# Expert stage of a one-core diffusion layer: twenty weight buffers, one 80-row scatter per expert, a last down product in the shape of the others

## The reference, cut to what matters

```python
def expert_choice_ffn(h, w_router, w_gate, w_up, w_down):
    cap = 2 * n // N_EXPERTS                       # 64 of 512 latent, 16 of 128 context rows per expert
    aff = softmax(h @ w_router)
    gates, idx = top_k(swapaxes(aff, 1, 2), cap)   # each expert picks its own rows
    xe = h[idx]
    ye = (silu(xe @ w_gate) * (xe @ w_up)) @ w_down * gates
    return zeros(n, d).at[idx].add(ye)
x = x + gate2 * expert_choice_ffn(h, ...)
y = rms_norm(x, g_final)
```

## Time and profile before

| | |
|---|---|
| device time, median of 3 runs | 1182.05 us |
| the profiled execution's own time | 1175.39 us |
| its span, first to last instruction | 1173.6 us |
| TensorE busy | 1104.6 us (94%) |
| VectorE busy | 449.3 us (38%) |
| ScalarE busy | 367.7 us (31%) |
| GpSimd busy | 200.1 us (17%) |
| DMA in the expert stage | 395 to 411 GB/s in nearly every slice of 29 us |
| the chain that ended last | PE 71%, DMA 16%, DVE 5% |

### The profile page before, as it was taken

The page is one execution under the profiler, slowest core; times in us unless marked ns, Lnnn a source line. Parts: engine busy times, 40 slices in busy tenths (PEclk is TensorE's granted clock), DMA queues, the critical chain, the costliest instruction groups (busy, mean ns, idle before and its releaser), DMA issues.

```text
span 1173.6 us, 28123 instructions
## 1 busy us (share of the span) xinstructions
PE 1104.6 (94%) x12399; PEld 797.6 (68%) x12399; DVE 449.3 (38%) x755; ACT 367.7 (31%) x818; POOL 200.1 (17%) x237
## 2 busy tenths in 40 slices
PE   6999999999999999999979999999999998999883
PEld 4679877778876777777857777777777555555540
DVE  4574458889957142244373110111111110101113
ACT  4333337777743212112244012222221121012103
POOL 1343450000000000010014022222222221121210
PEclk9999999999999999999997999999999999999997
DMA  9952242111052434549398999999999999999985
GB/s 365 305 199 72 73 94 47 31 35 34 9 221 69 153 137 144 179 155 358 126 367 312 411 395 397 395 395 396 396 396 395 396 399 411 398 385 397 379 319 196
DMA packets 117016, 303.46 MB, mean 259 GB/s; under 512 B 27817, under 2 KB 34818, under 8 KB 116386
## 3 DMA queue, kind: packets, MB, share of 16 engines
q1 hardware_dynamic: 104256, 273.21, 61.3%
q0 software_dynamic: 11472, 20.99, 6.9%
q10 hardware_dynamic: 1170, 7.48, 1.5%
HBM read 276.78 MB, written 19.64 MB: 253 GB/s over the span
## 4 chain that ended last, share of the span: by engine, by line
PE 71%; DMA 16%; DVE 5%; ACT 3%; issue 2%; SPq 2%; ACTq 0%; POOL 0%; DVEq 0%; POOLq 0%
PE ps L1196 29%; DMA late<-in_w_exp_down_dram 10%; PE ps L765 9%; PE ps L766 9%; PE ps L767 9%; PE ps L991 3%; PE ps L975 2%; DVE neg_max L1810 2%; SPq L710 2%; DMA raw<-in_w_exp_down_dram 2%; PE ps L1014 1%; DMA x_dram<-xn_p 1%; PE ps L1010 1%; DVE q_lo_t L1802 1%; DMA raw<-in_w_in_dram 1%
## 5 line engine op out<-in xcount | busy, mean ns | idle before, releaser
L1196 PE MATMUL ps<-late,xe 128*32 128x256 f32 x3648 | 200.3, 379 | 1.0 <-DMA late<-in_w_exp_gate_dram 1.0
L1196 PEld LDWEIGHTS ps<-late,xe 128*32 128x32 f32 x3648 | 133.6, 110 | 64.7 <-DMA late<-in_w_exp_gate_dram 2.9
L1563 ACT ACTIVATE xe<-xt,mod_t,scale 128x64 f32<-128x64 f32 x240 | 78.0, 413 | 184.8 <-DVE gates L2107 184.8
L2127 DVE SCALAR_TENSOR_TENSOR y_q<-ps,gates,gate_q 128x256 f32<-128x256 f32 x45 | 19.0, 478 | 303.2 <-PE ps L1196 303.2
L2349 POOL DMA_INDIRECT x_dram<-y_q,rows x45 | 71.4, 1587 | 373.6 <-DVE y_q L2127 364.4
L765 PE MATMUL ps<-w_hi,ht 128*128 128x512 f32 (+1 forms) x320 | 124.8, 390 | 0.0
L766 PE MATMUL ps<-raw_lo,ht 128*128 128x512 f32 (+1 forms) x320 | 121.8, 381 | 0.0
L767 PE MATMUL ps<-w_hi,ht 128*128 128x512 f32 (+1 forms) x320 | 121.8, 381 | 0.0
L1196 PE MATMUL ps<-late,ht 128*32 128x256 f32 x1920 | 109.4, 380 | 9.0 <-DMA late<-in_w_exp_down_dram 8.9
L1196 PEld LDWEIGHTS ps<-late,ht 128*32 128x32 f32 x1920 | 68.3, 110 | 47.4 <-DMA late<-in_w_exp_down_dram 14.8
L1196 PE MATMUL ps<-raw,xe 128*32 128x256 f32 x1632 | 92.2, 381 | 3.4 <-DMA raw<-in_w_exp_gate_dram 3.4
(11 more groups left out here) (308 smaller groups left out, 1687.1 us busy)
## 6 DMA issues: line engine op xcount, KB each, us to landing
late<-in_w_exp_down_dram SPq DMA_DIRECT2D x44, 1024.0 KB, 21.0
late<-in_w_exp_up_dram SPq DMA_DIRECT2D x40, 1024.0 KB, 18.4
late<-in_w_exp_gate_dram SPq DMA_DIRECT2D x36, 1024.0 KB, 18.8
raw<-in_w_exp_gate_dram SPq DMA_DIRECT2D x18, 1024.0 KB, 18.8
raw<-in_w_in_dram SPq DMA_DIRECT2D x16, 1024.0 KB, 5.7
raw<-in_w_exp_up_dram SPq DMA_DIRECT2D x16, 1024.0 KB, 18.4
raw<-in_w_exp_down_dram SPq DMA_DIRECT2D x14, 1024.0 KB, 21.2
raw<-in_w_mod_dram SPq DMA_DIRECT2D x12, 1024.0 KB, 6.9
```

Of the source, the lines that this page charges most:

```text
L1196: mm = pe.matmul(out[32 * q:32 * q + 32, :], x[:, k, :], columns_of(w, q), start=(k == 0), stop=(k == KD - 1))
L1563: a = act.activation(xe[:, e % 2, sets, k, :], xt[:, sets, k, :], ACT.Identity, scale=scale2[:, k, v:v + 1], bias=mod_t[:, 24 + k, v:v + 1])
```

## The change

- **Ring.** `ESLOT` is 20. The four new slots lie where token and routing buffers were, so their first chunks (16 to 19) wait until the rows of all experts are known (`s_rows`, 5) and the normed tokens are stored, no longer for chunks 0 to 3 to be used up.
- **Scatter.** The residual is scattered in whole rows: one indirect DMA per expert of 80 rows of 4 KB in place of three of 128 quarter rows. For it VectorE writes the result as [80 x 1024] (`y_row`): quarter q of set v goes from partitions 32q.. to partitions 32v.., in twelve multiplies of 32 (or 16) partitions x 256 columns in place of three of 128 x 256.
- **Hidden.** `hidden` becomes `activations`: multiply and turn by sets, in the order 0, 2, 1.
- **Down blocks.** They go set by set through all four chunks (before: two sets together, then the third). d15 is such a block too, in banks 0 to 2, and `s_front` counts its sets.
- **Order at the end.** d14 stands ahead of g15 and u15, where it stood between them. VectorE norms two tiles ahead of expert 15's `activations` and three behind it; the last rows are finished by quarters.
- **Loops.** None left on SP, ScalarE and VectorE. Several semaphores are merged or renamed, the DRAM copy of the gates goes, and g_final is loaded behind scatter 14.

```diff
-ESLOT = 16
+ESLOT = 20
+EXPERT_BLOCKS = [("g", 0), ("u", 0)]
+for _n in range(1, NE - 1):
+    EXPERT_BLOCKS += [("g", _n), ("d", _n - 1), ("u", _n)]
+EXPERT_BLOCKS += [("d", NE - 2), ("g", NE - 1), ("u", NE - 1), ("d", NE - 1)]
+FIRST_CHUNK = {b: 4 * n for n, b in enumerate(EXPERT_BLOCKS)}
...
-                                                                 32768, 40960, 49152))]
+                                                                 32768, 40960, 49152, 97280, 105472, 113664, 141312))]
...
+                    elif c == 16:
+                        sp.wait_ge(s_x2out, 16 * (NT + 1))
+                        sp.wait_ge(s_rows, 5)
+                    elif c == 19:
+                        sp.wait_ge(s_post, MODS_DONE + 1)
+                        sp.wait_ge(s_ss2, 2 * NT)
...
+                if kind == "d":
+                    last = n == NE - 1
+                    for at_set, v in enumerate((0, 2, 1)):
+                        pe.wait_ge(s_ht2, SETS * n + at_set + 1)
+                        out = bank(v, 0, 256) if last else bank(7, 0, 256) if v == 2 else bank(6, 256 * v, 256 * v + 256)
                         for k in range(KD):
                             c = c0 + k // 2
+                            if at_set == 0:
+                                pe.wait_ge(s_slot[c % ESLOT], expert_raw(c))
+                            mm = set_product(out, ht2[:, v], expert_chunk(c)[:, k % 2, :], quarter_columns, k)
...
+            def activations(n):
+
+                dve.wait_ge(s_half, done("u", n))
+                dve.wait_ge(s_silu2, n + 1)
+                for at_set, v in enumerate((0, 2, 1)):
+                    dve.tensor_tensor(h_t[:, v, :], h_t[:, v, :], bank(3 + v, 0, 256), ALU.mult).then_inc(s_dve, 1)
+                    dve.wait_ge(s_dve, own())
+                    t = dve.transpose(ht2[:, v, :, :].rearrange("p k b -> p (k b)"), h_t[:, v, :]).then_inc(s_ht2, 1)
+                dve.sem_inc(s_hm, 1)
+
+            def output_piece(n, v, q):
+                count = 32 if v < 2 else CAPC
+                src = slice(32 * q, 32 * q + count)
+                b, o = (v, 0) if n == NE - 1 else (6 + v // 2, 256 * (v % 2))
+                return dve.scalar_tensor_tensor(y_row[n % 2][32 * v:32 * v + count, 256 * q:256 * q + 256],
+                                                bank(b, o, o + 256, src), gates[src, n % EG, v:v + 1],
+                                                gate2_q[src, v // 2, :], ALU.mult, ALU.mult)
+
+            def output(n):
+
+                dve.wait_ge(s_half, done("d", n))
+                dve.wait_ge(s_xgt, n + 1)
...
                 for v in range(SETS):
-                    dve.scalar_tensor_tensor(y_q[:, e % 2, v, :], bank(6 + v // 2, 256 * (v % 2), 256 * (v % 2) + 256),
-                                             gates[:, e % EG, v:v + 1], gate2_q[:, v // 2, :], ALU.mult, ALU.mult)\
-                       .then_inc(s_yg, 1)
+                    for q in range(4):
+                        y = output_piece(n, v, q)
+                y.then_inc(s_yg, 1)
+
+            for n in range(NE - 1):
+                if n:
+                    output(n - 1)
+                tokens_turned(n + 1)
+                activations(n)
+
+            output(NE - 2)
...
-                for v in range(SETS):
-                    pool.indirect_dma_start(x1_quarters[:, :], bass.IndirectOffsetOnAxis(ap=rows[:, v, n:n + 1], axis=0),
-                                            y_q[:, n % 2, v, :], None, compute_op=ALU.add).then_inc(s_scat, 16)
+                pool.indirect_dma_start(x1_dram[:, :], bass.IndirectOffsetOnAxis(ap=rows_t[0:EROWS, n:n + 1], axis=0),
+                                        y_row[n % 2][0:EROWS, :], None, compute_op=ALU.add).then_inc(s_scat, 16)
```

More of the change, by code:

```diff
@@ L597, in expert_rows, with done @@
             return w[0, n, 2 * q * P:(2 * q + 2) * P, :].rearrange("(k p) n -> p k n", p=P)
[L599 to L618, removed]
+        def done(kind, n):
+            return DENSE_HALVES + FIRST_CHUNK[kind, n] + 4
         @block.sync
@@ L678, in _ @@
                         sp.dma_start(x_n[:, t, :], xs[t] if t < NTL else x_prompt[0]).then_inc(s_x[t], 16)
-            def weights(i, kind, e, c0, first):
+            for kind, n in EXPERT_BLOCKS:
                 for q in range(4):
-                    c = c0 + q
-                    if first and c == 2:
+                    c = FIRST_CHUNK[kind, n] + q
+                    if c == 2:
                         for t in range(NT):
@@ L1257, in side_product @@
-            def side_product(c, f, k):
-                pe.wait_ge(s_slot[c % ESLOT], expert_raw(c, NG))
-                w, flags = expert_chunk(c)[:, k % 2, f * NW:(f + 1) * NW], {"start": k == 0, "stop": k == KD - 1}
-                for v in range(SETS):
-                    mm = pe.matmul(bank(6 + f, rows=slice(32 * v, 32 * v + 32)), ht2[:, v, k, :], w, **flags)
-                if f and k % 2 == 1:
-                    mm.then_inc(s_half, 1)
-                elif f == 0 and k == KD - 1:
-                    mm.then_inc(s_front, 1)
@@ L1584, in _ @@
                                    bias=mod_t[:, 24 + k, v // 2:v // 2 + 1]).then_inc(s_xe0, 1)
-            groups(act, body)
+            for n in range(NE):
+                silu(n)
+                if n + 1 < NE:
+                    scaled(n + 1)
             def finish_rms(t):
@@ L2109, in hidden @@
[L2109 to L2122 removed]
+                dve.tensor_copy(gates[:, n % EG, :].unsqueeze(2), xg[:, b, :, 256 + n:257 + n]).then_inc(s_xgt, 1)
@@ L2131, in body @@
-            def body(i, first, last):
-                for e in range(EG):
-                    if e or not first:
-                        output(i, e - 1)
-                    if not last or e < EG - 1:
-                        tokens_turned(i, e + 1)
-                    else:
-                        dve.wait_ge(s_xgt, NE)
-                        for v in range(SETS):
-                            own_rows = slice(32 * v, 32 * v + (32 if v < 2 else CAPC))
-                            dve.tensor_copy(gate_z[own_rows, :], gates[own_rows, EG - 1, v:v + 1]).then_inc(s_rows, 1)
-                    hidden(i, e)
+                    for q in range(4):
+                        y = output_piece(n, v, q)
@@ new lines, in _ @@
+            finish(0)
+            finish(1)
+            activations(NE - 1)
+            for t in range(2, NT):
+                finish(t)
+            dve.wait_ge(s_scat, 16 * (NE - 2))
+            for at_set, v in enumerate((0, 2)):
+                dve.wait_ge(s_front, at_set + 1)
+                for q in range(4):
+                    output_piece(NE - 1, v, q).then_inc(s_dve, 1)
+            own(8)
+            dve.wait_ge(s_front, 3)
+            dve.wait_ge(s_xl2, 16)
+            for q in range(4):
+                output_piece(NE - 1, 1, q).then_inc(s_dve, 1)
+                dve.wait_ge(s_dve, own())
+                last_sums(q)
```

290 lines of the change are left out of this document (106 added, 184 removed).

## The result

| | before | changed |
|---|---|---|
| median of 4 runs each | 1180.07 us | 1202.03 us (1199.01 to 1204.45) |
| ratio | | 1.0182, 95% interval 1.0163 to 1.0200 |
| profiled execution / its span | 1175.39 / 1173.6 us | 1204.45 / 1202.6 us |

The change makes the kernel 1.8% slower. The profile of before and that of the changed kernel come from different chips, as experiment 1 shows, so a few microseconds between them need not come from the change. Both kernels run again on one chip (experiment 1) gave 1.0185 (1.0156 to 1.0213).

The account below looks back on a forecast made before the run. TensorE's own pace bound the kernel, with DMA close; lengthening the chain to `xe` would stall it. u15's end at 1169.5 plus a 31.8 tail made 1201.3 against 1173.6; +27.7 on median 1182.05 gave 1209.8 us, range 1174 to 1219.

Parts of the forecast that it names:

- chain longer by: Chain beside TensorE, from down block through output pieces to `xe`: 5.0 us longer a round, with 2.1 us to spare.
- TensorE stands: Start of the gate blocks g2 to g14: TensorE idles 2.9 us, 13 times, waiting for ScalarE's `xe`.
- a round without a fall of the clock: Expert rounds of three blocks: 34.0 us each instead of 31.08.
- falls: TensorE's clock drops to half behind the stalls in two rounds of three: 8.7 x 1.65 = 14.3 us, bounds 0 and 21.5.
- end of u15: End of expert 15's up block: at 1169.5 us, against 1138.1 before.
- The pieces are held: VectorE's output pieces each start only after the last ended: 0.508 us each, twelve 6.10 us; chance 0.75.
- the gain of slots and scatter: Four more weight slots issue chunks 8.8 us earlier and scatter relieves DMA, but no stall is left to fill.
- The tail: From the end of u15 to the span's end: 31.8 us, 3.7 less than before.
- The step from the profile to the median: Whole kernel: the 27.7 us added to the runs' median 1182.05, 6.7 above the profiled execution, giving 1209.8 us.
- 1, pieces not held: VectorE's pieces overlap: stall 1.45 us, round 32.5 us, span 7.9 us shorter, 1174.2 us; chance 0.13.
- 2, the lead pays: Chain stays hidden and the earlier weight chunks give 8.8 us: span 13.7 us shorter, 1168.4 us; chance 0.07.
- 3, the clock holds: No clock fall in any round: 1194.3 us, low end of the main case; no separate chance given.

Follow-up runs that it names:

- experiment 1: The kernel before and the changed kernel, both unedited, run again with profiles on one chip: ratios 1.0005 and 1.0185.
- experiment 3: Changed kernel, but pieces of experts 0 to 14 read bank, gates and gate row at the partitions they write (results wrong): 1182.95 us, ratio 1.0020.
- experiment 2: Changed kernel with VectorE turning the next expert's tokens before the twelve output pieces instead of after them: 1178.96 us, ratio 0.9993.
- experiment 6: Changed kernel with tokens turned before the pieces and the last expert's activations ahead of the first two finish steps: 1173.13 us, ratio 0.9990.
- experiment 7: The kernel of experiment 6 with 16 weight buffers instead of 20, same chip: 1179.72 us, ratio 1.0050.
- experiment 4: Changed kernel with experts 0 to 14 back to three 128x256 outputs and three quarter-row scatters: 1187.66 us, ratio 1.0055.

## Why the prediction was right, and where it only came out right

Forecast 1209.8 us, measured 1202.03; forecast +27.7 us on the spans, +29.0 between the first two profiles, which are of two chips, +22.0 between the medians, and +15.6 between the spans of experiment 1. Step by step, against the changed kernel's first profile:

| step | predicted | measured |
|---|---|---|
| twelve pieces, a round | 6.10 us | 5.92 |
| chain longer by | 5.0 | 4.6 |
| TensorE stands | 2.9, 13 times | 2.24, 13 times |
| a round without a fall of the clock | 34.0 | 33.5 |
| a fall costs | 1.65 | 1.68 |
| falls | 8.7 | 6 (4 in experiment 1) |
| first output | 670.8 | 679.6 |
| end of u15 | 1169.5 | 1167.9 |
| from there to the end | 31.8 | 34.7 |
| end of the span | 1201.3 | 1202.6 |

On one chip, by the profiles of experiment 1:

| | before | changed | difference | predicted |
|---|---|---|---|---|
| first output | 676.7 | 674.5 | -2.2 | 0 |
| a round without a fall of the clock | 32.1 | 33.5 | +1.4 | +2.9 |
| end of u15 | 1144.3 | 1159.5 | +15.2 | +31.4 |
| from there to the end | 35.1 | 35.4 | +0.3 | -3.7 |
| end of the span | 1179.4 | 1195.0 | +15.6 | +27.7 |

The ends of u15 are read from the starts and waits of d15:

```profile
1146.40 4.06 PE L1262 MATMUL ps<-late,ht 128*32 128x512 f32 x27 [2.09 <-DVE ht L2115]
1163.01 3.49 PE L1172 MATMUL ps<-late,ht 128*32 128x256 f32 x32 [3.46 <-issue]
```

**What was right.** The pieces are held (experiment 3), the chain through `xe` is what they lengthen (experiment 2), TensorE stands, and the waits for weights vanish. Taking the copies of the earlier trace rows as the measure, not the three wide outputs, decided this: the piece's pitch is 0.49 us (0.508 taken, 0.393 the other end). The page of the Trainium skill "VectorE: DVE Perf Modes", section "Two Vector instructions with no wait between them", says that an instruction in another group of 32 partitions than the one before is held; the runs agree, 5.92 against 5.01 us. By that section the inputs' move alone is enough, and they agree in this too: in nine of the eleven steps of a round only the inputs move, since the four pieces of a set are written to the same 32 partitions, and these nine are the steps that experiment 3 shortens most. That the gain of slots and scatter has nothing to fill follows from the missing waits; no run takes the four slots out of the changed kernel alone.

**What was too high.** The chain grew by 4.6 us, not 5.0, and its slack was 2.4 us, not the 2.1 taken; so a round was 0.5 us shorter, 6.2 in 13 (the stall is 0.7 shorter, and 0.2 of it is lost elsewhere in the round). And the clock fell in half of the rounds or fewer, another 4.2. Waits of the same 2.24 us were followed by a fall in some rounds and not in others, so the length of the wait alone doesn't tell.

**What was luck.** In the first table the first output is 8.8 us late. That isn't the change: experiment 1 has both kernels late on its chip, and experiment 6's kernel has 670.6 where no place is slow, as forecast. The loss is a slow place at the first gathers, with the half clock in it in some profiles. These 8.8 us of the chip and the 10.4 above cancel, so the end of u15 came out right by luck.

**What was missing.** The rows came from a chip without slow places, and the forecast holds for such a chip at most. On the chip of experiment 1 the slow place lengthens a round of the kernel before to 32.1 us, while in the changed kernel it lies under the stall, so a round costs 1.4 us and not the forecast 2.9 (31.1 against 33.5 would be 2.4). The kernels' spans differ by 15.6 us there, a little over half of the forecast 27.7. On a chip without slow places the changed kernel itself was never run.

**The tail** fell short by 2.9 us: d15 started 2.75 us behind u15, not 2.15, lost 1.7 us to the half clock rather than 1.1, and the end came 12.2 us behind GpSimd's last scatters, not 10.0. All of these 2.1 are GpSimd's closing drain, 7.67 us instead of 5.50 (below). The rest was 0.4 quicker. Of the 3.7 us promised for the tail, 0.8 came, and in experiment 1 nothing.

**The step from the profile to the median failed.** The forecast put the 27.7 us on the median of 1182.05, 6.7 above the profiled execution. That difference is most likely slow places: by the profile of before in experiment 1, 5.9 us at the first gathers and 1.1 in each of 12 rounds, largely made up by fewer waits for weights (5.8 us instead of 16.2). The changed kernel doesn't add those of the rounds to its own loss: its slow place lies under the stall for `xe`, as the round above shows, where TensorE starts 0.09 us behind `xe` though VectorE was told 2 us late. Without this step the forecast is 1175.39 + 27.7 = 1203.1, and 1202.03 was measured; but this nearness is luck too, since the first is a time without slow places and the second one with them.

**Two slips.** The prediction puts 21.9 us down to late weights, while TensorE's waits for them add up to 16.2. And a fall of the clock in every round gives 1217.0 by its own terms, not 1217.5.

**The rivals.** 1, pieces not held: experiment 3 comes near that case, with 1183, not 1174. Its round of 32.7 us is near the rival's 32.5 by other parts: a slow place of 1.2 us and a stall of 0.3, not a stall of 1.45. 2, the lead pays: it needs the chain out of the way. Experiments 6 and 7 show that the lead is then worth 6.6 us, not 8.8, and experiment 6 still only equals the kernel before. 3, the clock holds: so it did in 7 of 13 rounds, and in 9 of 13 in experiment 1.

Still open: what makes the slow places on some chips. That they need gathers is argued from the rounds that have none; the run without gathers fell on a chip that has no slow place. What the change costs on such a chip is open too.

## What to carry to other kernels

Before more instructions go onto an engine that is 38% busy, find the chain that they lengthen and its slack: 4.6 us more in a chain with 2.4 to spare cost 22 us, and moving one line (turn the tokens first) took the loss back. What a buffer or a lighter transfer gives shows only once nothing else holds the bound engine. And profile both kernels on one chip before a few us are put down to a cause.

## What the runs showed of the hardware

- A VectorE instruction on another group of 32 partitions than its predecessor starts 0.09 us later than one on the same group (0.49 against 0.40 us from start to start, at 32x256 fp32 from PSUM to SBUF; experiment 3). A move of the inputs alone is enough.
- Chips differ by some 0.5% for one kernel: 1174.1 against 1179.8 and 1180.7 us. On some, TensorE has slow places of 1.1 to 1.2 us in rounds with gathers, and one at the first gathers that made the first output 5.9 us later in the kernel before. The trace gives no wait for them; the count of matmuls in two microseconds does (21 against 44).
- GpSimd's drain at the end of the program took 7.67 us in the kernels that scatter by one instruction and gather in full, 5.50 in the kernel before, 5.26 with the three scatters in the changed kernel and 4.73 without the gathers. So it differs with the indirect DMAs that GpSimd has issued (15 scatters and 48 gathers, 45 and 48, 45 and 48, 15 and 12), and not simply with their number. It is on the path.
- The loads of `x_f`, 2.6 MB, behind weights still under way took 15.9 us from the first issue to the first tile's use (experiment 4; 14.7 in experiment 6), 4.0 with the weights landed (changed kernel).
